# Attention values from half-precision parts, with the weighting shared by two engines, in a two-layer hybrid decoder step

## The reference

```python
def shared_attention(qg, qpos, k, v, kpos, mask, slopes):
    s = jnp.einsum('btkgd,bnkd->bkgtn', qg, k).astype(jnp.float32) * (B_HD ** -0.5)
    s = s - slopes[None, :, :, None, None] * dist[:, :, None]
    p = masked_softmax(s, mask)
    o = jnp.einsum('bkgtn,bnkd->btkgd', p.astype(v.dtype), v)
...
    o = g[..., 0:1] * o_cmp + g[..., 1:2] * o_slc + g[..., 2:3] * o_win
```

## Time and profile before

| what | us |
|---|---|
| median of 3 runs (lowest to highest) | 2917.41 (2913.49 to 2924.06) |
| the profiled execution's own time | 2923.37 |
| its span, first to last instruction | 2921.7 |
| score stage in it | 714.9 to 1027.3 |
| TensorE busy over the span | 2741.7 (94%) |
| VectorE, ScalarE, GpSimd busy over the span | 1270.4, 1150.8, 352.8 |
| mean granted TensorE clock | 0.973 of full speed |

### The profile page before, as it was taken

The page is one execution under the profiler, slowest core; times in us unless marked ns, Lnnn a source line. Parts: engine busy times, 40 slices in busy tenths (PEclk is TensorE's granted clock), DMA queues, the critical chain, the costliest instruction groups (busy, mean ns, idle before and its releaser), DMA issues.

```text
span 2921.7 us, 47262 instructions
## 1 busy us (share of the span) xinstructions
PE 2741.7 (94%) x18103; PEld 1823.3 (62%) x18103; DVE 1270.4 (43%) x2097; ACT 1150.8 (39%) x1593; POOL 352.8 (12%) x530
## 2 busy tenths in 40 slices
PE   5888898997999998999999999899998999999997
PEld 3667666655555564666666666566665666666664
DVE  8254454324555636444444122532336444443123
ACT  4664654322666724444444111211124444443111
POOL 0320303323000000111111000011100111111000
PEclk9899999999999999999999999999999999999999
DMA  3222223363000031111111111111111111111111
GB/s 131 79 73 63 67 64 121 105 187 110 1 1 1 4 112 37 51 50 50 50 50 53 64 49 41 44 50 50 51 44 37 52 49 49 50 50 64 53 54 59
DMA packets 113483, 173.19 MB, mean 59 GB/s; under 512 B 16993, under 2 KB 83922, under 8 KB 112978
## 3 DMA queue, kind: packets, MB, share of 16 engines
q1 hardware_dynamic: 92610, 150.90, 16.1%
q0 software_dynamic: 3792, 12.58, 1.3%
q10 hardware_dynamic: 16960, 8.16, 1.0%
HBM read 161.47 MB, written 14.30 MB: 60 GB/s over the span
## 4 chain that ended last, share of the span: by engine, by line
PE 78%; DVE 8%; SPq 6%; ACT 4%; issue 3%; DMA 1%; ACTq 0%; DVEq 0%
PE PS L1726 61%; PE PS L2050 5%; PE PS L2064 2%; ACT xT L823 2%; SPq L534 2%; SPq L537 2%; DVE R L1184 2%; PE PS L1706 2%; PE PS L1759 1%; PE PS L2021 1%; PE PS L1827 1%; DVE hT L1189 1%; PE PS L2022 1%; SPq L464 1%; SPq L459 1%
## 5 line engine op out<-in xcount | busy, mean ns | idle before, releaser
L1726 PE MATMUL PS<-hT,R 128*128 128x344 f16 x10152 | 1487.3, 310 | 6.1 <-DVE R L510 4.9
L1726 PEld LDWEIGHTS PS<-hT,R 128*128 128x128 f16 x10152 | 992.4, 98 | 498.4 <-DVE R L510 3.3
L510 DVE SCALAR_TENSOR_TENSOR R<-W,R 128x1024 f16<-128x1024 f32 (+1 forms) x186 | 248.5, 1336 | 964.2 <-ACT R L504 963.7
L504 ACT ACTIVATE R<-W 128x1024 f16<-128x1024 f32 (+1 forms) x186 | 206.5, 1110 | 923.6 <-PE PS L1726 919.3
L1726 PE MATMUL PS<-R 128*128 128x344 f16 x3276 | 478.2, 309 | 0.0
L1726 PEld LDWEIGHTS PS<-R 128*128 128x128 f16 x3276 | 320.2, 98 | 157.6
L1622 DVE SCALAR_TENSOR_TENSOR R<-R 128x1024 f32<-128x1024 f32 x96 | 123.3, 1285 | 79.3 <-ACT R L1127 78.0
L2050 PE MATMUL PS<-R 128*64 128x256 f32 (+1 forms) x592 | 155.0, 391 | 1.1 <-ACT R L1023 0.9
L823 ACT ACTIVATE xT<-xT 64x1024 f32<-64x1024 f32 x64 | 124.8, 1950 | 57.2 <-DMA xT<-cmp_t 56.0
L723 POOL COPY R<-R 128x2 f32 x88 | 19.4, 220 | 1035.8 <-ACT R L1126 1035.8
L1624 DVE SCALAR_TENSOR_TENSOR R<-R 128x1024 f32<-128x1024 f32 x96 | 123.3, 1285 | 13.6 <-DVE R L1623 12.3
(11 more groups left out here) (290 smaller groups left out, 2551.7 us busy)
## 6 DMA issues: line engine op xcount, KB each, us to landing
W<-wk SPq DMA_DIRECT2D x154, 512.0 KB, 3.4
W<-wdn SPq DMA_DIRECT2D x32, 704.0 KB, 4.0
xT<-cmp_t SPq DMA_DIRECT2D x256, 64.0 KB, 1.9
xT<-x SPq DMA_DIRECT2D x16, 516.0 KB, 7.3
o_y<-hT SPq DMA_DIRECT2D x6, 688.0 KB, 3.5
o_win_s<-state_win POOLq DMA_DIRECT2D x1, 4088.0 KB, 24.0
R<-s_hgrn POOLq DMA_DIRECT2D x4, 512.0 KB, 5.5
o_hgrn_s<-R ACTq DMA_DIRECT2D x4, 512.0 KB, 3.2
```

Source lines behind the costliest of these rows:

```text
L504: act.activation(to[:, n, 0, 0:width], W[:, n, 0:width], ACT.Copy, scale=UNIT).then_inc(wh_here, 1)
L510: dve.scalar_tensor_tensor(to[:, n, 1, 0:width], W[:, n, 0:width], UNIT, to[:, n, 0, 0:width], ALU.mult, ALU.subtract).then_inc(w_split, 1)
L1726: ins = pe.matmul(wide(u)[:, m, :], weights[half], src[:, other, m * TW:(m + 1) * TW], start=(first and half == other == 0), stop=(last an ...
```

## The change

- Values are split ahead of the stage into a high and a low float16 part (`VP`, `VPC`), laid side by side, so that one product of 128 output rows gives the high part's result on one half of the partitions and the low part's on the other. ScalarE and VectorE take six instructions each for it.
- The weights, transposed, are split too: ScalarE copies them times 1,024 to float16, VectorE then subtracts that from the same PSUM bank, times 1,024, into a second float16 buffer (`low_part`). Each value product of a block becomes two float16 products, with the high and with the low weights.
- The two halves of the result are added: ScalarE copies one to `OTHER`, VectorE adds the other (`heads_sum`) into `mix`.
- GpSimd multiplies the weights of even units; its split of `mix` moves behind units 28, 36, 44 and 52.
- The selected scores' banks are handed over apart from the rest (`slc_full`, `slc_free`).
- TensorE computes the scores of unit 2m+5 ahead of the last two groups' value products of pair m, which before came behind them as the next pair's first step.

The diff, without the lines that declare semaphores:

```diff
@@ -223,7 +223,8 @@
...
         SS = [reg(17080 + n * 1728, 1728) for n in range(4)] + [xf[:, n * 1728:(n + 1) * 1728] for n in range(2)]
-        PT = reg(23992, 4, 4 * P)
+        PRODUCT = 1024.0
+        OTHER = reg(26608, 2 * P)
         NG, DG, RG = (reg(26552 + 18 * n, 6, 3) for n in range(3))
...
@@ -244,6 +245,9 @@
...
         KY = halves(reg(8256, 2048)).rearrange("p (c g n) -> p c g n", c=2, g=2)
+        PT = halves(reg(23992, 2048)).rearrange("p (t s n) -> p t s n", t=4, s=2)
+        VP = halves(reg(10320, 2048)).rearrange("p (c t g n) -> p c t g n", c=2, t=NC, g=2)
+        VPC = halves(reg(28736, P)).rearrange("p (g n) -> p g n", g=2)
         CX, CY = (halves(v).rearrange("p (g n) -> p g n", g=2) for v in (xf[:, 4096:4160], reg(28608, 64)))
...
@@ -441,6 +452,15 @@
...
         SCORES, TURNED = 6, 4
+        def by_pool(n):
+            return n % 2 == 0
+        def weigh_turn(n):
+            return sum(by_pool(k) == by_pool(n) for k in range(n))
         TURN_BANKS = (4, 5, 7)
...
@@ -705,10 +725,22 @@
...
             wait_full(pool, U_S + 7)
-            for k in range(HA):
+            def mix_parts(k):
                 pool.tensor_copy(H2[:, k, 0, :], mix[:, k, :]).then_inc(mix_hi, 1)
...
                 pool.tensor_tensor(H2[:, k, 1, :], mix[:, k, :], H2[:, k, 0, :], ALU.subtract).then_inc(mix_a, 1)
+            for n in range(len(units)):
+                i = units[n][0]
+                if by_pool(n):
+                    pool.wait_ge(rg_here, n + 1)
+                    for c, cols in spans(i):
+                        part = SS[n % SCORES][:, cols]
+                        ins = pool.tensor_scalar(part, part, RG[:, n % SCORES, c:c + 1], None, ALU.mult)
+                    ins.then_inc(pw_pool, 1)
+                if n in (28, 36, 44, 52):
+                    mix_parts((n - 28) // 8)
...
@@ -981,6 +1013,12 @@
...
             value_pages(act, 5, held)
+            act.wait_ge(kl_here, 12)
+            for g in range(2):
+                part = slice(64 * g, 64 * g + 64)
+                for c, values in enumerate((VSL, VWN)):
+                    act.activation(VP[:, c, :, g, part], values[:, :, part], ACT.Copy).then_inc(vh_here, 1)
+                act.activation(VPC[0:NCP, g, part], VCP[0:NCP, part], ACT.Copy).then_inc(vh_here, 1)
             wait_full(act, U_S + 6)
...
@@ -1003,9 +1041,9 @@
...
                 rows = slice(64 * half, 64 * half + 64)
+                other = slice(64 - 64 * half, 128 - 64 * half)
                 act.wait_ge(pv_full, m + 1)
-                act.activation(mix[rows, HA + j:HA + j + 2, i * P:(i + 1) * P],
-                               PS[rows, 6, 0:2 * P].rearrange("p (a b) -> p a b", b=P), ACT.Copy).then_inc(pv_free, 1)
+                act.activation(OTHER[rows], PS[other, 6, 0:2 * P], ACT.Copy, scale=1 / PRODUCT).then_inc(oth_here, 1)
...
@@ -1020,8 +1058,8 @@
...
                     act.wait_ge(t_full, turn + 1)
-                    act.activation(PT[:, turn % TURNED, 0:cols], PS[:, TURN_BANKS[turn % 3], 0:cols], ACT.Copy
-                                   ).then_inc(t_free, 1)
+                    act.activation(PT[:, turn % TURNED, 0, 0:cols], PS[:, TURN_BANKS[turn % 3], 0:cols], ACT.Copy,
+                                   scale=PRODUCT).then_inc(th_here, 1)
                 exponential(2 * m + 4)
...
@@ -1459,6 +1497,14 @@
...
                                                      ALU.mult, ALU.subtract).then_inc(ql_here, 1)
+                    dve.wait_ge(vh_here, 6)
+                    for g in range(2):
+                        part, to = slice(64 * g, 64 * g + 64), slice(64 - 64 * g, 128 - 64 * g)
+                        for c, values in enumerate((VSL, VWN)):
+                            dve.tensor_tensor(VP[:, c, :, g, to], values[:, :, part], VP[:, c, :, g, part], ALU.subtract
+                                              ).then_inc(vl_here, 1)
+                        dve.tensor_tensor(VPC[0:NCP, g, to], VCP[0:NCP, part], VPC[0:NCP, g, part], ALU.subtract
+                                          ).then_inc(vl_here, 1)
             wait_full(dve, U_S + 7)
...
@@ -1475,14 +1521,36 @@
...
                 i, j, half = units[n]
-                dve.wait_ge(sc_full, n + 1)
+                dve.wait_ge(slc_full, n + 1)
                 if n >= SCORES:
...
                 for c, cols in spans(i):
+                    if c == 2:
+                        dve.wait_ge(sc_full, n + 1)
                     tab = TABC[:, i, 0:NCP] if c == 0 else TAB[:, cols]
...
                                                    ALU.add, ALU.min, NG[:, n % SCORES, c:c + 1])
+                    if c == 1:
+                        ins.then_inc(slc_free, 1)
                 ins.then_inc(sc_free, 1)
+            def heads_sum(m):
+                i, j, half = units[2 * m]
+                rows = slice(64 * half, 64 * half + 64)
+                dve.wait_ge(oth_here, m + 1)
+                dve.scalar_tensor_tensor(mix[rows, HA + j:HA + j + 2, i * P:(i + 1) * P],
+                                         PS[rows, 6, 0:2 * P].rearrange("p (a b) -> p a b", b=P), 1 / PRODUCT,
+                                         OTHER[rows].rearrange("p (a b) -> p a b", b=P), ALU.mult, ALU.add).then_inc(pv_free, 1)
+            def low_part(m, g):
+                i = units[2 * m][0]
+                turn = group_at[m] + g
+                cols = 2 * P * len(blocks(i)[2 * g:2 * g + 2])
+                dve.wait_ge(th_here, turn + 1)
+                dve.scalar_tensor_tensor(PT[:, turn % TURNED, 1, 0:cols], PS[:, TURN_BANKS[turn % 3], 0:cols], PRODUCT,
+                                         PT[:, turn % TURNED, 0, 0:cols], ALU.mult, ALU.subtract).then_inc(t_free, 1)
...
@@ -1500,6 +1568,8 @@
...
                     dve.tensor_tensor(rg, rg, gate, ALU.mult).then_inc(rg_here, 1)
+                if by_pool(n):
+                    return
                 dve.wait_ge(rg_here, n + 1)
...
@@ -1514,8 +1584,16 @@
...
                 weighted(2 * m + 2)
-                biased(2 * m + 4)
-                weighted(2 * m + 3)
+                count = groups[units[2 * m][0]]
+                for g in range(count):
+                    if g == count // 2:
+                        biased(2 * m + 4)
+                    low_part(m, g)
+                    if g == 0 and m:
+                        heads_sum(m - 1)
+                    if g == count // 2:
+                        weighted(2 * m + 3)
+            heads_sum(len(units) // 2 - 1)
             dve.wait_ge(pv_full, len(units) // 2)
...
@@ -2010,7 +2088,7 @@
...
                 if n:
-                    pe.wait_ge(sc_free, n)
+                    pe.wait_ge(slc_free, n)
                 if n < 2:
...
@@ -2024,34 +2102,41 @@
...
                     lo = cols.start
+                    if c and n:
+                        pe.wait_ge(sc_free, n)
                     while lo < cols.stop:
...
                         keys = slice(key, key + end - lo)
-                        scores(psf[:, lo:end], KX[:, c, half, keys], KY[:, c, half, keys])
+                        ins = scores(psf[:, lo:end], KX[:, c, half, keys], KY[:, c, half, keys])
                         lo, key = end, key + end - lo
+                    if c == 0:
+                        ins.then_inc(slc_full, 1)
                 scores(psf[:, cmp], CX[:, half, 0:NCP], CY[:, half, 0:NCP]).then_inc(sc_full, 1)
...
                 bl = blocks(i)
-                rows = slice(64 * half, 64 * half + 64)
...
                         pe.wait_ge(pv_free, m)
+                    if g == m == 0:
+                        pe.wait_ge(vl_here, 6)
                     for b, (kind, t, _) in enumerate(bl[2 * g:2 * g + 2]):
-                        p = PT[:, turn % TURNED, 2 * b * P:2 * (b + 1) * P]
+                        high, low = (PT[:, turn % TURNED, n, 2 * b * P:2 * (b + 1) * P] for n in range(2))
                         if kind == "cmp":
-                            v, p = VCP[0:NCP, rows], p[0:NCP]
+                            v, high, low = VPC[0:NCP, half, :], high[0:NCP], low[0:NCP]
                         else:
-                            v = (VSL if kind == "slc" else VWN)[:, t, rows]
-                        ins = pe.matmul(PS[rows, 6, 0:2 * P], v, p, start=(g == b == 0), stop=(2 * g + b == len(bl) - 1),
-                                        skip_group_check=True)
+                            v = VP[:, ("slc", "win").index(kind), t, half, :]
+                        out = PS[:, 6, 0:2 * P]
+                        pe.matmul(out, v, high, start=(g == b == 0), stop=False, skip_group_check=True)
+                        ins = pe.matmul(out, v, low, start=False, stop=(2 * g + b == len(bl) - 1), skip_group_check=True)
                     return ins
-                pe.wait_ge(pw_here, 2 * m + 2)
+                for n in (2 * m, 2 * m + 1):
+                    pe.wait_ge(pw_pool if by_pool(n) else pw_here, weigh_turn(n) + 1)
                 for g in range(groups[i]):
...
```

(11 more changed lines are left out.)

## The result

The changed kernel takes 2892.41 us (2890.06 to 2892.66, 4 runs) where the kernel before takes 2920.24 beside it (2913.49 to 2924.06, 4 runs): ratio 0.9907, 95% interval 0.9893 to 0.9921. The forecast was 2892. Its profiled execution took 2892.66, with a span of 2890.9 against 2921.7. Of the 30.8 us between the spans the stage gives 26.8: it runs from 711.8 to 997.4, 285.6 us where the forecast had 285 and before it took 312.4. The last 0.9 lies behind the stage.

What follows compares the result with a forecast made beforehand. TensorE's stream bound the score stage; VectorE would pace it next: 246.7 work + 30.4 waits + about 5 opening + 3 splits = 285 against 312.4 us; 27 less, 2 left for the clock, so 2917.4 becomes 2892, range 2873 to 2921.

Steps and rivals of the forecast that it cites:

- forecast A: Score stage: VectorE paces it after the change, 25 us less, 2874 to 2908; chance 0.73.
- VectorE's work: Score stage: 183.1 - 3.8 - 34.0 + 90.5 + 10.9 = 246.7 us busy on VectorE.
- The four moved splits ... I count 3 us in all: GpSimd's splits of `mix` in chunks 4 to 1 run past their cover: 3 us, between 0 and 4 x 3.2.
- The waits: VectorE's waits in the stage: 0.95 us a pair, laid out for chunk 7, times 32 (30.4), plus about 5 at the opening.
- a dip of the clock: TensorE's clock at the stage's opening: 2 us left for it, turning 27 us less into 25.
- so I take 1.0: GpSimd's weighting: 1.0 ns per column, 1727 columns in some 2 us; bounds 1.01 and 4.4 ns.
- C: VectorE's gate and weighting of odd units: GpSimd locks VectorE out, 43 us at 4.4 ns per column, 2935; chance 0.08.
- the cover: Time before VectorE's next weighting, hiding GpSimd's: four low parts, a head sum and a bias, 4.8 us.
- Rival B: Score stage: the three-engine hand-over eats the gain, waits 1.6 to 1.8 us a pair, 2913 to 2919; chance 0.15.
- Rival D: TensorE in the stage: its clock falls to the lower level, about 3040 us if throughout; chance 0.04.
- clock 1.00 after the opening: Sign that the forecast is right: TensorE's clock at 1.00 in the stage; under 0.9 would show it wrong.
- The small chunks: Last chunks of the stage: the change loses there; chunk 0's pairs 4.25 us at least against 3.6, some 3 us.

Runs made afterwards that it cites:

- early splits: Changed kernel with GpSimd's four splits of `mix` behind units 4, 6, 8, 10, each once VectorE has weighted the odd unit: 2885.69 us, ratio 0.9879.
- the variant with 0.92 over 230 us: Changed kernel with VectorE weighting all units, GpSimd none, and splits of `mix` held until VectorE has weighted the odd unit: 2927.19 us, ratio 1.0024.

## Why the prediction was right

**TensorE** saves 294.5 - 222.9 = 71.6 us (forecast 69) and stops being the bound. VectorE paces the stage, as forecast A has it: TensorE waits for its low parts and sums (31.1 and 22.7 us), and without the low parts 64.5 us are gone.

**VectorE's work** was forecast at 246.7 and is 258.2, 11.5 more. The prices of low parts and head sums were right: 0.61 and 0.34 from one start to the next where the next instruction follows at once. Some are followed by a wait, and then their tail counts too; summed from each row's start to the next one's, or to its own end where VectorE then waits, both take 105.1 instead of 101.4. The other 8 are the weighting, whose rows add up to 40.9 instead of 34.0, and the gates: 8.7 us of both are GpSimd's splits, as the early splits show. The step that failed is "The four moved splits ... I count 3 us in all", between 0 and 12.8: 8.8 by the pairs. The overrun was worked out from the lengths, but a weighting that starts beside a split gives way for nearly all of it (3.01 instead of about 1), and the gate too.

**The waits** were forecast at 30.4 + 5 and are 285.6 - 258.2 = 27.4. In chunk 7 they are (35.3 - 31.85) / 3 = 1.15 a pair, near the 0.95 laid out; in chunks 5 to 2 only 0.3 to 0.5. One pair's waits were carried to 32 pairs, and in the middle chunks they are smaller. So the waits were put 8.0 too high, the work 11.5 too low, and the 3 for the splits stood as a term of their own: 11.5 - 8.0 - 3 is the half us between 285 and 285.6. The total is better than its terms, and that is luck. So is the last step to 2892: 2 us were left for a dip of the clock beside the 27 of the stage, but the dip (0.83 from 720 to 730) is inside the 285.6, so the stage gave 26.8 and not 25; against that the kernel before took 2920.24 beside the changed one and not 2917.4. The span given for A, 2874 to 2908, is not the sum of its terms either: with low parts and waits both at their upper or lower values they give about 2877 to 2920.

**GpSimd's weighting** failed by its rate: "so I take 1.0" a column; it is 5.14 us for 1,727 columns, 3.0. (The row of 2.14 that stands there as another product is a subtraction, the second step of a split.) That lies above the 2.8 from which C was said to decide, and C did not come: the cover was not the 4.8 counted, which was work alone. From 737.59 to VectorE's gate at 743.34 are 5.75, since VectorE also waits for scores in it (0.66 before 740.50) and takes a reciprocal before the gate. C's mechanism is real: its sign, a gate or weighting above 1 us beside GpSimd, did come at the four splits (3.01 in chunk 3) and cost the 8.8. From GpSimd's own weightings 0.6 us kept it away. The Trainium skill (GPSIMD Engine Reference, section 4.1) has GpSimd about twice as slow as VectorE for two inputs and roughly at line rate for one. Here the product with one tensor is the slower on GpSimd, 5.14 against 3.35 a unit, and VectorE's takes 1.38, so the page's order does not hold for these forms.

**Rival B** did not come: VectorE waits 10.4 before the low parts in the whole stage, 0.3 a pair, where B's sign was 1.5. Without either reordering of the scores waits of B's size appear, 20 and 33 us, but before the biases, for scores, which the prediction had in its layout of the waits and not under B. **Rival D** was put as a fall of the whole stage to the lower level. The clock falls in part: in the changed kernel in a few stretches from 910 on, at no cost that could be measured, and in the variant with 0.92 over 230 us at some 10 us. The sign "clock 1.00 after the opening" held only to 910. **The small chunks** lose 7.0 us in chunks 1 and 0, where some 3 were forecast for chunk 0 alone: 4.2 there, and 2.8 in chunk 1, of which 2.0 are a split. Chunk 0's pairs take 4.6, not 4.25. That bank 6 is free only after ScalarE's copy and VectorE's sum (22.7 us of TensorE's waits) may be why; a second bank for it was not tried, since all eight are in use.

## What to carry to other kernels

A change that relieves the bound is worth what the next engine lets through: sum that engine's work and its waits pair by pair, for large and small tiles apart. Look at the order of hand-overs too: here one of them, 32 us, outweighed the whole gain. Work moved to GpSimd was free here only while VectorE's instructions with all operands in SBUF stood clear of it, so place it behind those and in the longest stretches, and write down the margin. Two terms that miss in opposite directions can give a right total; check the terms.

## What the runs showed of the hardware

- GpSimd's multiplication by a column takes 2.84 us for 1,024 columns of float32, VectorE's the same in 0.75; as a product of two tensors, one of them a column read again, three pieces of 1,727 columns take 3.35 instead of 5.14.
- VectorE's gate (three columns, all in SBUF) and weighting stretch beside GpSimd (0.16 to 0.48 and 0.93, 1.38 to 2.18), its biases and low parts with an operand in PSUM do not (1.23 and 0.69 with GpSimd beside them or not).
- The granted clock of TensorE falls in parts of a stage in which it waits on VectorE (0.92 over 230 us at 175.5 busy), and products by zeros raised it (0.97 at 192.0 busy) and the kernel's speed with it.
